# Gates of three residual sums multiplied into the weights in the ring instead of into the sums

## The reference, cut to what matters

```python
sc = jax.nn.silu(c)
for i in range(DEPTH):                      # DEPTH = 2
    mod = sc @ w_ada[i] + b_ada[i]
    sh_m, sc_m, g_m, sh_f, sc_f, g_f = jnp.split(mod, 6, axis=-1)
    h = modulate(x, norm_mix[i], sh_m, sc_m)
    y = moba_attention(...) if i == 0 else short_conv(...)   # ends in "@ w_o" / "@ w_out"
    x = x + g_m[:, None, :] * y
    h = modulate(x, norm_ffn[i], sh_f, sc_f)
    x = x + g_f[:, None, :] * swiglu(h, w_gate_up[i], w_down[i])   # ends in "@ w_down"
return x
```

## Time and profile before

| what | value |
|---|---|
| time, median of 3 runs | 1275.48 us (1275.18 to 1276.98) |
| the profiled execution: its time, its span | 1276.19 us, 1274.4 us |
| PE busy | 1232.6 us, 97% |
| DVE busy | 947.2 us, 74% |
| ACT busy | 717.7 us, 56% |
| chain that ended last | PE 88%, DVE 5%, ACT 4% |
| DMA | 263.78 MB, mean 207 GB/s |

### The profile page before, as it was taken

How to read it: one execution, slowest core, us unless ns; L and a number is a source line. 1 busy time by engine, 2 the same in 40 slices (tenths; PEclk the granted TensorE clock), 3 DMA queues, 4 the chain that set the end, 5 groups by cost and what they waited for, 6 DMA issues and landing times.

```text
span 1274.4 us, 23473 instructions
## 1 busy us (share of the span) xinstructions
PE 1232.6 (97%) x9891; PEld 1147.7 (90%) x9891; DVE 947.2 (74%) x1263; ACT 717.7 (56%) x1048; POOL 16.5 (1%) x28
## 2 busy tenths in 40 slices
PE   6999999999999999999998998999999999999998
PEld 6989799999899879999988996999998998999997
DVE  5887379888768677999976656799986676677453
ACT  7833377655664667666657455654455544644432
POOL 0021000000000000000000000000000000000000
PEclk9999999999999999999999999999999999999999
DMA  9450277776557256789662534799975356575540
GB/s 322 159 199 4 67 265 232 264 250 205 206 199 264 71 181 212 248 275 305 232 246 83 184 133 132 249 348 359 339 257 199 133 199 198 205 258 199 197 167 34
DMA packets 163875, 263.78 MB, mean 207 GB/s; under 512 B 5869, under 2 KB 98233, under 8 KB 163770
## 3 DMA queue, kind: packets, MB, share of 16 engines
q1 hardware_dynamic: 160586, 259.54, 59.6%
q10 hardware_dynamic: 3184, 2.73, 0.7%
HBM read 261.17 MB, written 1.05 MB: 206 GB/s over the span
## 4 chain that ended last, share of the span: by engine, by line
PE 88%; DVE 5%; ACT 4%; issue 2%; DMA 1%; SPq 0%; DVEq 0%; ACTq 0%
PE ps L1096 24%; PE ps L1067 15%; PE ps L1069 15%; PE ps L1068 15%; PE ps L2322 2%; PE ps L835 2%; PE ps L1082 2%; PE ps L836 1%; PE ps L837 1%; PE ps L1083 1%; PE ps L1084 1%; DVE wlo L611 1%; PE ps L815 1%; ACT whi L605 1%; DMA arena<-in_w_ada_dram 1%
## 5 line engine op out<-in xcount | busy, mean ns | idle before, releaser
L611 DVE TENSOR_TENSOR wlo<-ring,whi 128x2048 fp32r<-128x2048 f32 x194 | 443.3, 2288 | 103.2 <-ACT whi L605 103.0
L1067 PE MATMUL ps<-ghi,whi 128*128 128x256 f32 x1600 | 448.3, 280 | 0.6 <-DVE wlo L611 0.6
L1068 PE MATMUL ps<-glo,whi 128*128 128x256 f32 x1600 | 446.7, 279 | 0.0
L1069 PE MATMUL ps<-ghi,wlo 128*128 128x256 f32 x1600 | 446.6, 279 | 0.0
L605 ACT ACTIVATE whi<-ring 128x2048 fp32r<-128x2048 f32 x194 | 370.6, 1915 | 85.3 <-PE ps L1096 54.6
L1067 PEld LDWEIGHTS ps<-ghi,whi 128*128 128x128 f32 x1600 | 300.3, 188 | 2.0 <-DVE wlo L611 0.8
L1068 PEld LDWEIGHTS ps<-glo,whi 128*128 128x128 f32 x1600 | 299.8, 187 | 1.2
L1069 PEld LDWEIGHTS ps<-ghi,wlo 128*128 128x128 f32 x1600 | 300.4, 188 | 0.0
L1096 PE MATMUL ps<-whi,yhi 128*128 128x512 f32 x480 | 158.6, 395 | 3.1 <-DVE ylo L1977 1.3
L1096 PE MATMUL ps<-wlo,yhi 128*128 128x512 f32 x480 | 156.1, 390 | 0.0
L1096 PE MATMUL ps<-whi,ylo 128*128 128x512 f32 x480 | 155.9, 390 | 0.0
(11 more groups left out here) (307 smaller groups left out, 1569.8 us busy)
## 6 DMA issues: line engine op xcount, KB each, us to landing
arena<-in_w_ada_dram SPq DMA_DIRECT2D x48, 1024.0 KB, 5.9
ring<-in_ff_w_up_dram SPq DMA_DIRECT2D x44, 1024.0 KB, 7.7
ring<-in_w_gate_up_dram SPq DMA_DIRECT2D x44, 1024.0 KB, 7.1
ring<-in_ff_w_down_dram SPq DMA_DIRECT2D x10, 2048.0 KB, 8.0
ring<-in_w_down_dram SPq DMA_DIRECT2D x10, 2048.0 KB, 8.1
ring<-in_od_w_qkv_dram SPq DMA_DIRECT2D x6, 2048.0 KB, 8.4
ring<-in_w_qkv_dram SPq DMA_DIRECT2D x6, 2048.0 KB, 8.0
ring<-in_w_in_dram SPq DMA_DIRECT2D x6, 2048.0 KB, 8.1
```

Of the source, the lines that this page charges most:

```text
L611: e.tensor_tensor(shaped(WLO[i % NB], k), v, shaped(WHI[i % NB], k).bitcast(F32), ALU.subtract).then_inc(S["w_lo"], 1)
L1067: e.matmul(o, wh, h[0][:, k, :], start=k == 0, stop=False)
L1068: e.matmul(o, wh, h[1][:, k, :], start=False, stop=False)
L1069: x = e.matmul(o, wl, h[0][:, k, :], start=False, stop=k == NK - 1)
```

## The change

- `GATED` names three sums, `o2`, `out2` and `down3`. Their gate is no longer applied in `dve_residual`, which adds straight from PSUM for them; `down2` keeps the old way.
- For each half of those weights (4 of `o2`, 4 of `out2`, 11 of `down3`) DVE now multiplies the half by the gate in place in the ring (`gate_half`), directly behind the `split_lo` of the half before. It first waits for the gate row and for the landing of the chunk. ACT's `split_hi` of that half waits for it.
- The last four steps of the modulation move from tiles 5, 7, 9, 11 of `ffn3` to tiles 2, 4, 6, 8 of `cin`, with their loads, `adahi`, `adalo`, two pairs of matmuls and two additions to the gate row. The last gate row is thus complete at the end of `cin`.
- Two semaphores of the first stack are merged into one, with the same meaning.

```diff
--- before.py
+++ after.py
@@ -113,10 +113,12 @@
     ("qkv", [("tile", i) for i in (2, 3, 4, 5)]),
     ("ffn1", [("tile", i) for i in (5, 7, 9, 11, 13, 15, 17)] + [("rows", i) for i in (0, 4, 6, 8, 12)]),
     ("ffn2", [("tile", i) for i in range(3, 17)] + [("rows", i) for i in range(0, 12, 2)]),
-    ("cin", []),
-    ("ffn3", [("tile", i) for i in (5, 7, 9, 11)]),
+    ("cin", [("tile", i) for i in (2, 4, 6, 8)]),
+    ("ffn3", []),
 ]
 MOD_Q = {0: 0, 1: 1, 3: 2, 4: 3}
+
+GATED = {"o2": (0, 0), "out2": (1, 0), "down3": (1, 1)}
 
 
 
@@ -596,10 +598,24 @@
                 first, self.made = self.made, max(self.made, end)
                 return range(first, end)
 
+        gated_halves = [i for i, (n, _, _, _) in enumerate(halves) if chunks[n][0][0] in GATED]
+
+        def gate_half(e, i):
+
+            n, v, _, _ = halves[i]
+            l, f = GATED[chunks[n][0][0]]
+            for h in range(2):
+                e.wait_ge(*read_out(("ada", 12 * l + 6 * f + 4 + h)))
+            e.wait_ge(S[f"ring{n % NS}"], landed[n])
+            e.tensor_tensor(c3(v, 2), c3(v, 2), rep(GB[l][f], 2), ALU.mult).then_inc(S["w_gated"], 1)
+
         def split_hi(e, which):
             for i in which:
                 n, v, k, _ = halves[i]
-                e.wait_ge(S[f"ring{n % NS}"], landed[n])
+                if i in gated_halves:
+                    e.wait_ge(S["w_gated"], gated_halves.index(i) + 1)
+                else:
+                    e.wait_ge(S[f"ring{n % NS}"], landed[n])
                 if i >= NB:
                     e.wait_ge(S["w_used"], i - NB + 1)
                 e.activation(shaped(WHI[i % NB], k), v, ACT.Copy).then_inc(S["w_hi"], 1)
@@ -610,6 +626,8 @@
                 e.wait_ge(S["w_hi"], i + 1)
                 e.tensor_tensor(shaped(WLO[i % NB], k), v, shaped(WHI[i % NB], k).bitcast(F32),
                                 ALU.subtract).then_inc(S["w_lo"], 1)
+                if i + 1 in gated_halves:
+                    gate_half(e, i + 1)
 
         def first_piece(x, p):
             return x[:, 1024 * p:1024 * p + 1024]
@@ -771,14 +789,14 @@
         SHIFT = [None] * 4 + [modc[:, l, 2 * q, :] for l, q in TWO]
 
         SUM_OF = [None, "ev_out", "down0", "od_out", "down1", "o2", "down2", "out2", "down3"]
-        GATE_OF = [None] * 5 + [GB[l][f] for l, f in TWO]
+        GATE_OF = [None] * 6 + [GB[0][1], None, None]
 
         def x_ready(k, n, h):
 
             if k == 0:
                 return S[f"x{n}"], 16
             if GATE_OF[k] is not None:
-                return S["x_gated"], 4 * (k - 5) + 2 * n + h + 1
+                return S["x_gated"], 2 * n + h + 1
             return read_out(("sum", SUM_OF[k], n, h))
 
 
@@ -1764,15 +1782,14 @@
             split_lo(e, w.go())
             mixed(2)
             e.wait_ge(S["consts_in"], 16)
-            e.memset(SS[:, :, :, 0:1], 0.0).then_inc(S["ss_zero"], 1)
+            e.memset(SS[:, :, :, 0:1], 0.0).then_inc(S["scanned"], 1)
             for j in range(4):
                 e.wait_ge(*read_out(("sg", 0, j // 2)))
                 for n in range(2):
                     x = e.tensor_tensor_scan(SS[:, j, n, 1:129], ones, W0[:, j, 128 * n:128 * n + 128], 0.0,
                                              ALU.mult, ALU.add)
             x.then_inc(S["scanned"], 1)
-            e.wait_ge(S["ss_zero"], 1)
-            e.wait_ge(S["scanned"], 1)
+            e.wait_ge(S["scanned"], 2)
             mid = SS[:, :, :, 64]
             e.tensor_scalar(c3(KS, 4), mid, KAPPA, None, ALU.mult).then_inc(S["ss_mid"], 1)
             e.tensor_scalar(c3(NKS, 4), mid, -KAPPA, None, ALU.mult).then_inc(S["ss_mid"], 1)
```

## The result

| | before | after |
|---|---|---|
| time, median of 4 runs each, beside each other | 1276.23 us (1275.18 to 1278.91) | 1285.56 us (1284.65 to 1286.66) |
| ratio after / before | | 1.0063, interval 1.0043 to 1.0082 |
| the profiled execution: time, span | 1276.19 us, 1274.4 us | 1286.66 us, 1284.9 us |
| PE, DVE, ACT busy | 1232.6, 947.2, 717.7 us | 1238.0, 979.3, 717.4 us |

The two medians differ by 9.3 us; the interval of the ratio allows 5.5 to 10.5. The rows of the changed kernel that answer to those shown before follow. First the timeline of DVE at the end of cin and in out2; L627 is the parting, L610 the new multiplication.

A forecast was written before the change was run, and what follows sets the result against it. PE was taken to bound cin, out2 and ffn3, with DVE work free if delivered in time. Out2's 12.0 us delay less the gains gave + 7.6 on 1276.19; adjusted to the median, 1283.2, 8-in-10 range 1278.5 to 1288.5.

The forecast's parts named there:

- The backlog, stage by stage: In cin and out2, 23.1 us added on DVE exceed the fillable 8.5 us of waits; out2's residual starts 13.3 us late.
- The price of L610: Multiplying a half by its gate on DVE costs the parting's 2.21 us start to start, bounds 1.1 and 4.4.
- Rival 3: In cin, multiplying a half costs another amount: 1.1 us each gives 1278.8, 4.4 gives 1292; chance 0.05.
- PE's waits: Between 1057 and 1082 us PE stands for about 2.9, 1.9 and 4.9 us, first on `adalo`, then on `wlo`.
- o2: At the end of o2's sum, dropping the gate multiplications gains 1.31 us at n = 0 and 0.72 at n = 1.
- The price of 0.59 for a quarter: The skill's PSUM and SBUF cycle charges save 0.59 us per quarter instead of 0.72, making the time 1283.8.
- down3 and the end: Eleven multiplications in ffn3 cost 0; the kernel's last quarter gains 0.72 us, four matmuls leaving ffn3 gain 0.9.
- The transposes of out2: Behind out2's late residual, the first transposes come at 1089.7, 12.0 us late, set by DVE rather than PE's matmuls.
- rival 2: PE's clock falls in the new waits around out2: at most + 5.3 us, 1288.5, more likely part of it; chance 0.10.
- The sum: Whole kernel: + 12.0 - 0.72 - 2.03 - 0.72 - 0.9 gives + 7.6 us on 1276.19, 1283.8; forecast 1283.2.
- Rival 1: Late DVE fills all 20.2 us of idle time in cin and out2: - 2.8 us, 1272.7; chance 0.10.

## Why the prediction was right

The forecast was 1283.2, the measured median 1285.56; the direction, the place and the mechanism are those of the prediction.

- **The backlog, stage by stage: right.** On the trace's axis the changed kernel is 0.42 us behind at the start of cin. Less that, the partings of halves 12 to 15 stand at 1055.2, 1063.7, 1071.3 and 1079.0, forecast 1055.1, 1063.7, 1071.3 and 1079.0; the residual at 1086.0, forecast 1086.1. It worked because every duration came from a row and because the idle time that the alternation with ACT makes was counted again in every stage, however late DVE is, and only that which PE's pace leaves was filled.
- **The price of L610: right.** 2.284 us, 2.21 from start to start, in place and with the repeated gate row: the parting's price, neither 1.1 nor 4.4. Rival 3 is out.
- **PE's waits: right.** 2.82, 1.55 and 4.64 us against 2.9, 1.9 and 4.9, the first on `adalo`.
- **o2: right.** Forecast 2.03 (1.31 and 0.72), measured 2.23 (1.45 and 0.78). The price of 0.59 for a quarter, set against the row's 0.72, is not borne out. At the first transposes PE's wait, 1.70 in the earlier trace rows, is 0.26 (forecast 0.4).
- **down3 and the end: right.** No PE wait in ffn3, eleven multiplications hidden in 101.04 busy of 156 us. The gain behind out2 is 1.95, forecast 1.62 (0.72 for the last quarter and 0.9 for the four matmuls).
- **The transposes of out2: one term short.** Forecast 12.0 late; measured 1091.08 - 0.42 - 1077.68 = 13.0. The step that failed is "PE's matmuls (6.8 us from 1081.3) are done by 1088.2, so DVE sets this": at half the clock for part of them the 30 matmuls took 9.33 us and ended at 1091.1, and PE set it. That was rival 2, given 0.10, which allowed for at most 5.3 us. With PE kept busy 1.2 to 1.4 us of the piece come back. The rows could not say that waits of 2.9, 1.9 and 4.9 us were harmless, so a part of this belonged in the sum. The Trainium skill, TensorE: Matmul & The Clock Gate, "Why this matters for your kernels", cited there, warned of long gaps between bursts; the trace agrees at the wait of 4.64 us, in which the clock went to 0.50.
- **The rest of the miss** is in the first stack, 2.7 us in the profiled execution, and nothing that the prediction could have read: the trace of before was at 1.00 throughout.
- **The sum: close in part by luck.** The pieces add up to + 7.8 us against + 7.6 forecast, but the sum had no term for the clock. Without its 1.4 us in out2 they would be + 6.4 (an estimate): the backlog came out 0.4 smaller and the gains 0.8 larger than forecast, and the clock made up for both.
- **Rival 1** ("DVE soaks it up") is out: ACT's parting stood behind ACT's scaling in every late stage, with 0.28 to 1.11 us of idle time ahead of the partings of halves 12 to 15.

One estimate that the prediction did not make, and that the parts allow: with the multiplications alone in cin, 8.8 us meet only the 5.05 us of idle time in the last stages (1.90 + 3.15), since the 2.52 + 0.93 lie ahead of them; 8.8 - 5.05 - 1.31 = 2.4 us late, measured 1.6 to 2.0. With the steps alone (14.2 of the 23.1 us, against 8.5 of idle time that PE's pace leaves), 14.2 - 8.5 = 5.7, measured 5.1, of which 0.5 is the late landing.

## What to carry to other kernels

In this kernel work on an engine with idle time was free only up to the idle time that the bounding engine's pace leaves. Idle time that comes from a handshake with a second engine came back in every stage and absorbed nothing, so count the cycle of the handshake, not the busy share. And look at what stands behind the moved work in the same queue, a buffer's release, a PSUM bank's read-out or a load's order: in each of the three places where they were tried (cin, the end and the beginning of ffn2) these steps delayed another of them. Of a bundle of edits, run the parts alone: here one part gained 2 us and hid in a loss of 9.

## What the runs showed of the hardware

- A multiplication of two fp32 tensors of 128 x 2048, in place and with one operand repeated, takes DVE the 2.28 us of a plain one; GpSimd took 4.52 to 6.68 us for it, 4.97 in the median.
- DVE's operations with two SBUF inputs did not run beside GpSimd's multiplication: 4.9 to 5.0 us instead of 0.75 for three step operations. Neither did the scaling of 128 x 128 by a column (9.05 us for two, 0.3 each otherwise). A multiplication that reads PSUM kept its 0.68 us.
- PE's clock fell to 0.50 in out2 of the changed kernel, in a wait of 4.64 us, and did not fall there once PE had matmuls to do. Shorter waits went both ways: behind 2.58 us (PE kept busy later), 2.99 us (o2 and down3 gated) and 3.10 us (end of ffn2) it was at 0.50, behind 2.82 us (the change, at `adalo`) and another 3.10 us (no sum gated) at 1.00. What decides between them no run here shows.
- It fell too in the first stack, in the traces of six of the fourteen programs, between 70 and 80 or between 130 and 145 us or at both, and set most of the spread between executions of one kernel: 1275.0 to 1275.4 against 1279.9 to 1281.1 us for the same program.
